# Hybrid decoder trunk on one core: layer 2's experts from place 12 on in one 3 MB transfer each, their order made behind expert 0, the last experts' steps rearranged

## The reference

```python
g_prob = softmax(t @ w_group); g_w, g_sel = top_k(g_prob, 1)        # 1 of 4 groups
e_logits = (t @ w_expert)[of the chosen group]
e_val, e_sel = top_k(e_logits, 2)                                   # 2 of its 8 experts
e_w = softmax(e_val) * g_w
for e in range(32):
    he = silu(t @ w_gate[e]) * (t @ w_up[e])                        # 1024 -> 256
    y = y + combine[:, e, None] * (he @ w_down[e])                  # 256 -> 1024
x = x + g_f * y
```

## Time and profile before

| | |
|---|---|
| median of 3 runs | 690.08 us (689.83 to 690.11) |
| profiled execution, its own time | 690.19 us |
| its span, first to last instruction | 688.5 us |
| TensorE's mean granted clock | 0.987 |
| PE busy | 626.9 us (91%) |
| DVE, ACT, POOL busy | 251.1, 120.1, 60.5 us |
| moved by DMA | 273.32 MB, mean 397 GB/s |
| chain that ended last | PE 80%, DMA 11%, issue 5% |

### The profile page before, as it was taken

How to read it: one execution, slowest core, us unless ns; L and a number is a source line. 1 busy time by engine, 2 the same in 40 slices (tenths; PEclk the granted TensorE clock), 3 DMA queues, 4 the chain that set the end, 5 groups by cost and what they waited for, 6 DMA issues and landing times.

```text
span 688.5 us, 12940 instructions
## 1 busy us (share of the span) xinstructions
PE 626.9 (91%) x4790; PEld 383.7 (56%) x4790; DVE 251.1 (36%) x668; ACT 120.1 (17%) x312; POOL 60.5 (9%) x187
## 2 busy tenths in 40 slices
PE   4889899999899999999999999999999867998885
PEld 1445465554455555556888788886544324454452
DVE  1014433222222223245689495247332302222223
ACT  4013530000000000014244333237100000000003
POOL 7000021101001001100000000001111100001000
PEclk9999999999999999999999999999999979999998
DMA  9999999999999999999997989963999999999992
GB/s 354 417 420 422 428 421 433 430 428 431 433 430 428 430 428 426 423 420 421 418 422 282 413 343 426 422 277 127 390 425 420 427 427 421 425 426 423 425 419 97
DMA packets 27259, 273.32 MB, mean 397 GB/s; under 512 B 3141, under 2 KB 3653, under 8 KB 4937
## 3 DMA queue, kind: packets, MB, share of 16 engines
q1 hardware_dynamic: 27208, 272.65, 94.7%
HBM read 271.59 MB, written 1.05 MB: 396 GB/s over the span
## 4 chain that ended last, share of the span: by engine, by line
PE 80%; DMA 11%; issue 5%; ACT 1%; DVE 1%; SPq 1%; ACTq 0%; POOL 0%; DVEq 0%
PE bank L835 71%; DMA ring<-in_ada_w_dram 9%; PE bank L1043 6%; DMA ring<-in_exp_w_dram 2%; PE bank L1218 1%; PE bank L1526 1%; SPq L510 0%; ACT hx L2039 0%; PE bank L1380 0%; PE bank L1387 0%; DVE ye L2080 0%; ACT reg_b L1845 0%; ACT reg_a L1710 0%; ACTq L177 0%; DVE ye L2077 0%
## 5 line engine op out<-in xcount | busy, mean ns | idle before, releaser
L835 PE MATMUL bank<-ring,xh 128*64 128x256 f32 (+2 forms) x2496 | 306.0, 429 | 34.9 <-issue 33.9
L835 PEld LDWEIGHTS bank<-ring,xh 128*64 128x64 f32 (+1 forms) x2496 | 169.6, 134 | 132.2 <-issue 75.9
L2077 DVE TENSOR_TENSOR reg_c<-reg_c,bank 128x128 f32<-128x128 f32 x58 | 16.7, 288 | 183.0 <-ACT reg_c L1733 96.5
L763 POOL COPY xh<-reg_a 128x256 f32 (+1 forms) x106 | 41.2, 399 | 410.9 <-PE bank L835 287.2
L835 PE MATMUL bank<-reg_b,ring 128*128 128x256 f32 x256 | 57.2, 380 | 0.4 <-ACT reg_b L1890 0.4
L1043 PE MATMUL bank<-ye,reg_b 32*128 32x512 f32 (+1 forms) x432 | 52.8, 599 | 0.0
L835 PEld LDWEIGHTS bank<-reg_b,ring 128*128 128x128 f32 x256 | 48.0, 190 | 7.1 <-issue 0.9
L2077 DVE TENSOR_TENSOR ye<-bank,reg_c 128x512 f32<-128x512 f32 (+1 forms) x60 | 40.2, 670 | 29.5 <-PE bank L835 29.0
L2341 DVE COPY xh<-bank 128x128 f32<-128x128 f32 x58 | 16.6, 285 | 93.0 <-PE bank L835 93.0
L835 PE MATMUL bank<-ring,cact 128*32 128x512 f32 (+1 forms) x320 | 34.0, 535 | 16.5 <-DMA ring<-in_ada_w_dram 16.4
L1733 ACT ACTIVATE reg_c<-bank 128x128 f32<-128x128 f32 x32 | 8.9, 277 | 203.9 <-PE bank L835 203.9
(11 more groups left out here) (212 smaller groups left out, 457.0 us busy)
## 6 DMA issues: line engine op xcount, KB each, us to landing
ring<-in_exp_w_dram SPq DMA_DIRECT2D x41, 2048.0 KB, 20.3
ring<-in_exp_w_dram SPq DMA_DIRECT2D x20, 3072.0 KB, 16.0
ring<-in_ada_w_dram SPq DMA_DIRECT2D x48, 1024.0 KB, 17.7
ring<-in_exp_w_dram SPq DMA_DIRECT2D x44, 1024.0 KB, 21.0
ring<-in_w_qkv_dram SPq DMA_DIRECT2D x12, 1024.0 KB, 16.3
ring<-in_w_o_dram SPq DMA_DIRECT2D x4, 1024.0 KB, 8.4
gu_spare<-in_exp_w_dram SPq DMA_DIRECT2D x1, 2048.0 KB, 20.3
hx<-in_exp_w_dram SPq DMA_DIRECT2D x2, 1024.0 KB, 19.5
```

Source lines behind the costliest of these rows:

```text
L763: nc.gpsimd.tensor_copy(xe[:, b, k0:k1, t * CAP:(t + 1) * CAP], hS[:, k0:k1, bass.ds(off, CAP)])\
L835: return nc.tensor.matmul(o_, l_, r_, start=start, stop=stop)
L2077: return nc.vector.tensor_tensor(o_, a_, b_, op)
```

## The change

- `STAT` goes from 7 to 8: place 7 is fixed as expert 7, the pairs are places 8 to 19, the singles 20 to 31. `UNITS` is now (0), (1), (2), (3), (7), pair (8, 9), (4), pair (10, 11), (5), pair (12, 13), (6), pairs (14, 15), (16, 17), (18, 19), and (20) to (31); still 26 units.
- SP issues gate and up of place 7 ahead of its wait for the order. Places 7 to 11 come in two transfers each as before, places 12 to 29 whole, and 30 and 31 in two transfers again.
- `order_rows` moves behind hidden of expert 0. DVE keeps the row (`keep_order`) behind expert 0's product and does `places_by_rows` in unit 1; `count_beyond` moves from unit 0 to behind unit 1's product.
- The last unit gets functions of its own: on PE down of unit 24 comes ahead of hidden of unit 25, and the rows of units 22, 23 and 24 are added one by one between these steps.

```diff
-STAT = 7
+STAT = 8
-UNITS = [(0,), (1,), (2,), (3,), LIGHTS[0], (4,), LIGHTS[1], (5,), LIGHTS[2], (6,)] + LIGHTS[3:] \
+UNITS = [(0,), (1,), (2,), (3,), (7,), LIGHTS[0], (4,), LIGHTS[1], (5,), LIGHTS[2], (6,)] + LIGHTS[3:] \
+WHOLE = (STAT + 4, E - 2)
...
-            def whole_expert(L, e, s, freed):
+            def whole_expert(L, e, s, freed, down_freed):
                 sp.wait_ge(S("ring_free", s), freed)
-                sp.wait_ge(S("down_free", s), freed)
+                sp.wait_ge(S("down_free", s), down_freed)
...
+            e = STAT - 1
+            gate_up(1, e, *exp_at(1, e))
             sp.wait_ge(S("off_ready"), 3)
-            e = expert_of(STAT)
-            gate_up(1, e, *exp_at(1, STAT))
-            for p in range(STAT, E):
+            for p in range(STAT - 1, WHOLE[0]):
+                if p + 1 < WHOLE[0]:
+                    following = expert_of(p + 1)
+                    gate_up(1, following, *exp_at(1, p + 1))
+                down_part(1, e, *exp_at(1, p))
+                e = following
+                if p == STAT:
+                    sp.wait_ge(S("tab_full"), 2)
+                    sp.wait_ge(S("ovf_ready"), 2)
+                    down_part(1, last, SPARE, 0)
+            for p in range(*WHOLE):
+                s, turn = exp_at(1, p)
+                whole_expert(1, expert_of(p), s, turn, down_turn(1, s, turn))
+            e = expert_of(WHOLE[1])
+            gate_up(1, e, *exp_at(1, WHOLE[1]))
+            for p in range(WHOLE[1], E):
                 if p + 1 < E:
                     following = expert_of(p + 1)
                     gate_up(1, following, *exp_at(1, p + 1))
                 down_part(1, e, *exp_at(1, p))
                 e = following
-                if p == STAT + 1:
-                    sp.wait_ge(S("tab_full"), 2)
-                    sp.wait_ge(S("ovf_ready"), 2)
-                    down_part(1, last, SPARE, 0)
...
+            def last_unit():
+                u = NU - 1
+                turn_he_of(1, u - 1, 0)
+                rows_unit(u - 3, 0)
+                down_unit(u - 1, 0, True)
+                hidden_unit(u, 1)
+                rows_unit(u - 2, 1)
+                turn_he_of(1, u, 1)
+                rows_unit(u - 1, 0)
...
-                pe.wait_ge(S("hS_dve"), 2 * len(BY_DVE))
-                mm(order_at, ones[0:E, :], order_diag, True, True).then_inc(S("counts"), 1)
+                mm(order_at, ones[:, :], order_diag, True, True).then_inc(S("counts"), 1)
...
                 else:
+                    order_rows()
                     pe.wait_ge(S("diag_ready"), 2 * T + 1)
...
+            def keep_order():
+                dve.wait_ge(S("counts"), 3)
+                nc.vector.tensor_copy(order_kept, order_at).then_inc(S("counts_read"), 1)
+                dve.wait_ge(S("counts_read"), 3)
...
                 if u == 1:
+                    places_by_rows()
                     dve.wait_ge(S("tab_ready"), 2)
...
                 if u == 0:
+                    keep_order()
+                if u == 1:
                     count_beyond(1)
```

More of the change, by code:

```diff
@@ L230, in program @@
         order_f = in_alibi(E)
+        order_kept = in_alibi(3 * E)
         ones = sb("ones", [P, P])
@@ L321, in program @@
         spread = ye[:, 1, 2 * P:4 * P].rearrange("p (v q) -> p v q", v=2)
[L322 to L325, removed]
+        chosen = ye[:, 1, 2 * P:2 * P + E]
+        of_place = ye[:, 1, 2 * P + E:2 * P + 4 * E].rearrange("p (f n) -> p f n", f=3)
+        order_diag = ye[:, 1, 2 * P + 4 * E:2 * P + 7 * E].rearrange("p (f n) -> p f n", f=3)
+        of_place_sum = ye[:, 1, 2 * P + 7 * E:2 * P + 7 * E + 3]
         Ssb = xe[:, 0, :, :].rearrange("p k c -> p (k c)")[:, 0:SEQ]
@@ L577, in later_experts @@
                         s, turn = exp_at(L, first + u)
-                        whole_expert(L, first + u + i * R, s, turn + i)
+                        whole_expert(L, first + u + i * R, s, turn + i, turn + i)
                 e = first + rounds * R
@@ L1087, in second_hidden @@
                 turn_he_of(L, 0, 0)
+                if L:
+                    pe.wait_ge(S("counts_read"), 3)
                 gu = gate_up_w(s).rearrange("p (g k j f) -> p k j g f", g=2, k=KC, j=2)
@@ L1227, in expert_unit @@
                 down_unit(u - 1, 1 - b, u >= 3)
[L1228 to L1231, removed]
+                if b:
                     rows_unit(u - 3, 0)
                     rows_unit(u - 2, 1)
+            def last_unit():
[7 more added lines that the diff above has]
+                rows_unit(u - 1, 0)
             def last_rows(L):
@@ L1274, in later_experts @@
                 else:
-                    for u in range(2, NU):
+                    for u in range(2, NU - 1):
                         expert_unit(u)
+                    last_unit()
                 n_ovf = beyond(pe, L)
@@ L1281, in later_experts @@
                 down(bank[3], down_w(s), 1, 0, 256).then_inc(S("dn_ready", L), 1)
-                if L:
-                    add_rows_of(L, n - 3, 1)
                 down(bank[1], down_w(s), 1, 256, 512).then_inc(S("dn_ready", L), 1)
-                add_rows_of(L, n - 2, 0)
+                if L == 0:
+                    add_rows_of(L, n - 2, 0)
                 with pe.If(n_ovf < 1):
@@ L1647, in _ @@
             gather(1)
-            order_rows()
             for e in range(2):
@@ L1765, in expert_unit @@
             def expert_unit(u):
+                if u == NU - 1:
+                    act.wait_ge(S("dn_ready", 1), u)
                 act.wait_ge(S("gu_ready", 1), u + 1)
@@ L2247, in route @@
                     take_gathered(L)
-                else:
-                    places_by_rows()
             def take_gathered(L):
@@ L2269, in order_experts @@
                 then(tt(place_of[:, free], others, moved, ALU.add))
[L2270 to L2273, removed]
+                then(nc.vector.tensor_scalar(chosen, place_of, own_part, None, ALU.is_equal))
@@ L2274, in order_experts @@
+                tt(of_place[:, 0, :], chosen, of_expert, ALU.mult)
+                then(tt(of_place[:, 1:3, :], offc.rearrange("p (t n) -> p t n", t=T),
+                        chosen.unsqueeze(1).broadcast_to([P, T, E]), ALU.mult))
                 then(nc.vector.tensor_reduce(of_place_sum, of_place, AX, ALU.add))
-                tt(order_diag, ident[0:E, 0:E].unsqueeze(1).broadcast_to([E, 3, E]),
-                   of_place_sum.unsqueeze(2).broadcast_to([E, 3, E]), ALU.mult).then_inc(S("diag_ready"), 1)
+                tt(order_diag, ident[:, 0:E].unsqueeze(1).broadcast_to([P, 3, E]),
+                   of_place_sum.unsqueeze(2).broadcast_to([P, 3, E]), ALU.mult).then_inc(S("diag_ready"), 1)
@@ L2278, in places_by_rows @@
+            def keep_order():
+                dve.wait_ge(S("counts"), 3)
+                nc.vector.tensor_copy(order_kept, order_at).then_inc(S("counts_read"), 1)
+                dve.wait_ge(S("counts_read"), 3)
             def places_by_rows():
-                dve.wait_ge(S("counts"), 3)
-                then(nc.vector.tensor_scalar(order_f[0:1, :], order_at[0:1, 0:E], 1.0 / RANKS, None, ALU.mult))
+                then(nc.vector.tensor_scalar(order_f[0:1, :], order_kept[0:1, 0:E], 1.0 / RANKS, None, ALU.mult))
@@ L2282, in places_by_rows @@
                 nc.vector.tensor_copy(order_i[:, :], order_f[0:1, :]).then_inc(S("off_ready"), 1)
[L2283 to L2287, removed]
@@ L2288, in places_by_rows @@
-                then(stt(pair_first, pair_step, second, pair_first, ALU.mult, ALU.add))
+                nc.vector.tensor_copy(off_at, order_kept[0:1, E:3 * E]).then_inc(S("off_ready"), 1)
+                nc.vector.tensor_scalar(lanes, order_kept[:, 0:E], of_lane[:, 0:1], None, ALU.add)
+                pairs = order_kept[:, STAT:STAT + 2 * NLP].rearrange("p (n x) -> p x n", x=2)
+                then(tt(pair_step, pairs[:, 1, :], pairs[:, 0, :], ALU.subtract))
+                then(stt(pair_first, pair_step, second, pairs[:, 0, :], ALU.mult, ALU.add))
@@ L2412, in expert_unit, with last_unit @@
                     take_ye(1, u - 1, 1)
+            def last_unit():
+                u = NU - 1
+                take_heT(1, u - 1, 0)
+                match_unit(u - 2)
+                dve.wait_ge(S("rows_added", 1), u - 3)
+                share_unit(u - 2, 1)
+                match_unit(u - 1)
+                dve.wait_ge(S("rows_added", 1), u - 2)
+                share_unit(u - 1, 0)
+                take_ye(1, u - 1, 0)
+                gate_he(1, u, 1)
             def expert(L, e, b, ahead_rows=False, next_rows=False):
@@ L2495, in later_experts @@
                 else:
-                    for u in range(NU):
+                    for u in range(NU - 1):
                         expert_unit(u)
+                    last_unit()
                 n_ovf = beyond(dve, L)
                 take_heT(L, n - 1, 1)
[L2500 to L2505, removed]
+                if L == 0:
```

(2 more changed lines are left out.)

## The result

| | before | after |
|---|---|---|
| median | 690.1 us (689.83 to 690.52) | 722.9 us (722.14 to 723.6) |
| profiled execution, its own time | 690.19 | 722.14 |
| span | 688.5 | 720.4 |
| TensorE's mean granted clock | 0.987 | 0.969 |

The ratio is 1.0475, with a 95% interval of 1.0462 to 1.0487: slower by 32.8 us, where 35.2 were forecast. The profiled executions, on which all that follows rests, differ by 31.9 us, as the one of the changed kernel is the fastest of its four. The bytes moved are the same 273.32 MB, PE's instructions the same 4790.

A forecast was written before the change was run, and what follows sets the result against it. The prediction took the DMA stream of weights as the bound. Its terms, +0.2 - 1.5 + 32.9 + 3.6 = +35.2 us, gave 725.4 on the profiled 690.19, or 725.3 beside the median, range 714 to 735.

The forecast's parts named there:

- term (c): Layer 2 weight stream: whole experts also wait for down_free, so the queue runs dry ahead of places 16 to 22, +32.9 us.
- (a): Start of layer 2: fixed place 7 and the order made behind expert 0 cost +0.2 us, bounds -0.2 to +0.5.
- (b): Layer 2 weight stream: one transfer in place of two for 18 experts saves 0.08 us each, -1.5 us in all.
- The restart: Within each hole: issue into an empty queue until landings go at full rate, 3.4 us, bounds 2.7 and 3.7.
- The clock: Within the holes: PE's matmuls run slower behind its waits, 1.6 us at hidden(9) and 2.3 three times.
- (d): Tail: place 29 lands whole, so PE ends 10.4 us behind the last byte instead of 6.8, +3.6 us.
- the queue never runs dry: Rival for layer 2's stream: no holes, 688.9 us with the tail absorbed or 692.5 with it; chance 0.05.
- the clock stays full: Rival for PE's work behind the holes: same holes without clock loss, 8.5 us less, 716.8 us; chance 0.13.
- half throughout: Rival for PE behind the holes: half clock through all of hidden and down, +9.6 us, 734.9 us; chance 0.10.
- The fixed cost per transfer: Rival for the stream: each of 18 transfers dropped saves 2.7 us, 49 us less, 641.6 us; chance 0.01.
- a late order: Rival at SP's loop: order late from DVE's longer unit 1, each us a us of stream; no separate chance given.

The follow-up runs named there:

- none whole: Changed kernel with places 7 to 31 all in two transfers, keeping fixed place 7, later order and new last unit: 693.7 us.
- the six and five merged ones: Six: changed kernel with only places 24 to 29 whole, 693.7 us; five: kernel before with only places 23 to 27 whole, 691.0 us.
- the clock kept: Changed kernel with products of constants put into PE's waits ahead of hidden of units 9, 12, 13 and 14: 717.6 us.
- pairs in two transfers: Changed kernel with the pairs' places 12 to 19 in two transfers again, only places 20 to 29 whole: 701.9 us.

## Why the prediction was right

The measured 722.9 us lies 2.4 from the forecast 725.3, and the mechanism of term (c) is the one that the runs show: one exchange of down and hidden on PE, with the same transfers, took 24.7 us away. The spans of the two profiled executions differ by 31.9, 3.3 less than forecast, and this is the sum of the terms as measured, 0.3 - 1.4 + 29.4 + 3.6; that the medians come 0.9 nearer is chance. Term by term:

- **(a), +0.2.** +0.3 between single executions (none whole), which can't be told from nothing. DVE's order of operations came as said: the order was ready at about 483.4, needed at 486.5.
- **(b), -1.5.** Whole experts land 7.30 us apart in a full queue, the two transfers of an expert 4.91 + 2.47: 0.08 us per merged transfer, 1.4 in all. (The last weights came 0.46 us earlier for six and 0.57 for five merged, between single executions.) A queue that has run dry costs more: each restart took 2.5 to 4.1 us beyond the transfer's 7.3, in all runs together. The Trainium skill has a fixed cost of about 2.0 us per transfer (DMA: Bandwidth & Descriptors, Anatomy of one DMA), for transfers that GpSimd issues; here SyncE issues them, and no such cost is in the stream of a full queue. The prediction also called on that page's advice to coalesce, but this is for many small transfers, and 1 and 2 MB are not small: no run here speaks against it.
- **(c), +32.9, measured 29.4.** Place by place 5.1, 11.7, 11.7, 4.4 were forecast and 4.3, 10.4, 11.8, 2.8 measured. Two parts of it were too large. The restart was 3.4 in the forecast and 2.8, 2.8, 3.1 and 2.7 in the changed kernel: the lone transfers' rows were nearer than the row that I took. The clock was put at 1.6 and three times 2.3, and was 1.3, 1.4, 2.6 and 1.8. Together they make up the 3.5 us.
- **(d), +3.6, measured 3.6.** From 687.5, when place 29 has landed, PE works without a wait to its end at 712.7, 25.2 us, which is the sum that was forecast. But the share of each edit is less simple. The old last unit with whole transfers gives 9.9, the new one without any 10.3, both together 10.5, against 6.9: two edits that each cost 3.0 to 3.4 alone, and hardly more together. With 29 whole PE is so late that it never waits for place 30's down, and the 40 matmuls there take 5.39 us; the new last unit by itself has the wait of 3.1 us and 6.93.

Of the rivals, "the queue never runs dry" falls with the holes; "the clock stays full" and "half throughout" fall with the clock's rows (6.94, 8.07 and 7.32 us where 5.5 and 11.0 would be the ends). The fixed cost per transfer falls with the six and five merged ones, and a late order with the run that has none whole. TensorE's clock was 0.50 from 590 to 598 while PE waited and 0.51 in its first microseconds of work behind that, and 1.00 through 540 to 630 where PE was given work to wait with. The Trainium skill has the clock's default as throttled, released by activity (TensorE: Matmul & The Clock Gate, Part 1): the trace agrees.

The expectations did worse than the prediction where a wait of PE was new: none of them (1.9 for the last unit, 3 for place 29) counted the half clock behind a wait of 3.1 and 6.6 us, though the prediction had that term.

## What to carry to other kernels

Merging two transfers also merges their waits: the merged one starts when the later of its slots' releases has come, and that release can stand behind a wait for the very weights that are next in line. Before merging, follow for each slot who used it last and what its releasing instruction waits for; with four slots and users that take two one behind the other, there was no slack here, while single users left plenty. And the part of a transfer that is needed first arrives only with the whole, which matters for the last few, where nothing behind them can make it up.

## What the runs showed of the hardware beyond what I expected

- A merged transfer is worth 0.08 us of stream where the queue is full, and a queue that has run dry costs 2.5 to 4.1 us to restart (3.1 MB landing 9.8 to 11.4 us after issue).
- The half clock multiplies small waits: a wait of 3.1 us for one transfer at the end cost 1.5 us more in the 40 matmuls behind it, one of 6.6 us cost 1.9. Shorter ones mostly cost nothing (5.39 us behind a wait of 2.64 at 643 in the changed kernel), but once did (7.08 behind 1.98 at 653 with the clock kept).
- Restarts differ by up to 1.6 us with nothing in view that explains it. With the clock kept, place 18 landed 1.2 us later after issue than in the changed kernel, with PE busy with constants all the while, but place 20 0.3 us sooner with constants beside most of it. With pairs in two transfers place 22 took 11.2 us with no constants at all. This stays open.
